# Two-layer hybrid decoder trunk on one core: value products issued for four attention units at a time in seven of sixteen steps

## The reference

```python
o = jnp.einsum('bngrqk,bnkgd->bnqgrd', (p / den).astype(v.dtype), vb)
```

## Time and profile before

| | us |
|---|---|
| three timed runs | 1310.58, 1310.74, 1311.07 (median 1310.74) |
| the profiled execution, its own time | 1306.06 |
| its span, first to last instruction | 1304.3 |

### The profile page before, as it was taken

How to read it: one execution, slowest core, us unless ns; L and a number is a source line. 1 busy time by engine, 2 the same in 40 slices (tenths; PEclk the granted TensorE clock), 3 DMA queues, 4 the chain that set the end, 5 groups by cost and what they waited for, 6 DMA issues and landing times.

```text
span 1304.3 us, 24577 instructions
## 1 busy us (share of the span) xinstructions
PE 1268.8 (97%) x8714; PEld 1182.7 (91%) x8714; DVE 763.3 (59%) x2339; ACT 643.5 (49%) x1777; POOL 368.9 (28%) x427
## 2 busy tenths in 40 slices
PE   4999999999999999999999999999999999999997
PEld 4998998988799999999989999899999899987997
DVE  5745453554772545666546666456775466668825
ACT  6445354454751445555446555456554456555312
POOL 2311142140301021212214932215832118610110
PEclk9999999999999999999999999999999999999999
DMA  5101012031546202101112311202310213215723
GB/s 203 39 19 50 26 54 85 18 98 37 173 148 202 98 25 54 40 25 25 51 50 65 86 58 36 65 26 83 98 44 19 65 39 91 84 31 138 212 98 129
DMA packets 101223, 97.29 MB, mean 75 GB/s; under 512 B 30704, under 2 KB 87536, under 8 KB 101104
## 3 DMA queue, kind: packets, MB, share of 16 engines
q1 hardware_dynamic: 101104, 95.73, 24.5%
HBM read 79.46 MB, written 16.25 MB: 73 GB/s over the span
## 4 chain that ended last, share of the span: by engine, by line
PE 85%; DVE 5%; issue 4%; DMA 3%; ACT 1%; SPq 1%; POOL 1%; DVEq 0%; ACTq 0%; POOLq 0%
PE j_bank L1162 59%; PE o_bank L1305 7%; PE t_bank L1284 6%; PE s_bank L1271 5%; PE j_bank L1249 3%; PE s_bank L1273 2%; DMA w_raw<-in_w_qkv 1%; PE o_bank L1162 1%; PE t_bank L1162 1%; DMA gate<-in_positions 1%; PE s_bank L1162 1%; DVE xr L1809 1%; DVE probs L1658 1%; DMA w_raw<-in_w_out 1%; DVE probs L1651 0%
## 5 line engine op out<-in xcount | busy, mean ns | idle before, releaser
L1162 PE MATMUL j_bank<-w_hi,ht_hi 128*128 128x384 f32 (+1 forms) x1312 | 445.0, 339 | 4.3 <-ACT v L1418 2.4
L1162 PE MATMUL j_bank<-w_lo,ht_hi 128*128 128x384 f32 (+1 forms) x1312 | 432.8, 330 | 0.0
L1162 PE MATMUL j_bank<-w_hi,ht_lo 128*128 128x384 f32 (+1 forms) x1312 | 432.7, 330 | 0.0
L1162 PEld LDWEIGHTS j_bank<-w_hi,ht_hi 128*128 128x128 f32 x1312 | 248.5, 189 | 16.2 <-issue 9.5
L1056 POOL TENSOR_TENSOR w_lo<-w_raw,w_hi 128x768 fp32r<-128x768 f32 (+1 forms) x60 | 104.6, 1744 | 550.9 <-ACT w_hi L1395 475.3
L1404 ACT ACTIVATE probs<-probs,stat 128x256 f32<-128x256 f32 (+1 forms) x512 | 231.0, 453 | 48.6 <-DVE stat L1663 46.7
L1162 PEld LDWEIGHTS j_bank<-w_lo,ht_hi 128*128 128x128 f32 x1312 | 248.8, 190 | 0.0
L1162 PEld LDWEIGHTS j_bank<-w_hi,ht_lo 128*128 128x128 f32 x1312 | 248.4, 189 | 0.0
L792 ACT COPY probs_t<-t_bank 128x256 f32<-128x256 f32 (+1 forms) x128 | 58.0, 453 | 282.2 <-PE o_bank L1305 276.5
L1395 ACT ACTIVATE w_hi<-w_raw 128x768 fp32r<-128x768 f32 (+1 forms) x120 | 88.5, 764 | 84.2 <-PE j_bank L1162 42.6
L1305 PE MATMUL o_bank<-probs_t,v 128*64 128x128 f32 x1600 | 116.4, 282 | 1.5 <-DVE probs_t L792 0.9
(11 more groups left out here) (170 smaller groups left out, 1849.4 us busy)
## 6 DMA issues: line engine op xcount, KB each, us to landing
w_raw<-in_w_qkv SPq DMA_DIRECT2D x64, 384.0 KB, 3.5
coef<-coef_dram SPq DMA_DIRECT2D x96, 128.0 KB, 3.0
w_raw<-in_w_gate SPq DMA_DIRECT2D x32, 256.0 KB, 3.3
mix_dram<-xr SPq DMA_DIRECT2D x12, 512.0 KB, 3.9
w_raw<-in_w_out SPq DMA_DIRECT2D x16, 384.0 KB, 3.7
qk<-mix_dram SPq DMA_DIRECT2D x12, 512.0 KB, 5.3
xr<-in_x SPq DMA_DIRECT2D x8, 512.0 KB, 7.2
out<-xr SPq DMA_DIRECT2D x7, 512.0 KB, 2.7
```

The source lines that it names most:

```text
L1162: last = pe.matmul(to, a(x_, kt), b(y_, kt), start=(start and kt == kts[0] and x_ == y_), stop=(stop and kt == kts[-1] and x_ == 1))
```

## The change

Three functions are added and two places use them.

- `by_fours(s)`: true for steps 0, 1, 2 (layer 0 without its last) and for steps 6, 9, 12, 15 (pattern 2).
- `values_at(s, a)`: which units get their value products in pair (s, a). For units of a step by fours, the pairs in which the older scheme would have taken units 0 and 1, 4 and 5, 8 and 9, or 12 and 13 take none, and the next pair takes all four. The products themselves, their order and their number stay.
- The copies of turned units need four places now. In pattern 2 only side 1 is used, so the unused half of `probs_t` serves (`own_place`). In layer 0 the two further places lie in `ot[3]` (`turned_place`).
- The copy's wait in such a step is for the unit four before it, not two. For the first two units of a pattern 2 step it stays at two.

The scores, transposes, fills, pieces, `store_ot`, all DMAs and all of DVE's, ACT's and POOL's instructions stay in number and order.

```diff
+def by_fours(s):
+    return s.p == 2 if s.layer == 1 else not s.last
+
+def values_at(s, a):
+    b, u = unit_before(s, a, V_BACK)
+    if b is None or (by_fours(b) and u % 4 == 0):
+        return []
+    return [(b, n) for n in range(u - 2 if by_fours(b) else u, u + 2)]
+
+def own_place(s, u):
+    return u // 2 % 2 if by_fours(s) and s.layer == 1 else 1
...
+        def turned_place(s, u):
+            if by_fours(s) and s.layer == 0 and u % 4 >= 2:
+                return ot[GROUPS - 1][:, 0, :].rearrange("p (a b c) -> p a b c", a=2, b=4)[:, u % 2, :, :]
+            return probs_t[:, u % 2, :, :]
+
...
-            if i >= 2:
+            if by_fours(s) and (u >= 4 or s.layer == 0):
+                if i >= 4:
+                    eng.wait_ge(summed, i - 3)
+            elif by_fours(s) and u >= 2:
+                eng.wait_ge(summed, UNITS * s.t + u - 3)
+            elif i >= 2:
                 eng.wait_ge(summed, i - 1)
...
-            to = probs_t[:, i % 2, :, :].rearrange("p (j e) q -> p j e q", e=2)
+            to = turned_place(s, u).rearrange("p (j e) q -> p j e q", e=2)
+            if by_fours(s) and s.layer == 1:
+                at = own_place(s, u)
+                return copy(to[:, :, at:at + 1, :], src[:, :, 1:2, :])
...
-                                         v[:, s.t % 2, n - 1 + side, :], probs_t[:, i % 2, 2 * j + side, :],
+                                         v[:, s.t % 2, n - 1 + side, :],
+                                         turned_place(s, u)[:, 2 * j + (own_place(s, u) if side == 1 else 0), :],
...
-                        for b, u in [unit_before(s, slot, V_BACK) for slot in pair]:
-                            if b:
-                                times_v(b, u)
+                        for b, u in values_at(s, a):
+                            times_v(b, u)
```

## The result

| | before | after |
|---|---|---|
| timed runs, median (lowest to highest) | 1310.66 (1310.21 to 1311.07, 4 runs) | 1301.52 (1300.11 to 1303.58, 4 runs) |
| the profiled execution, its own time | 1306.06 | 1303.58 |
| its span | 1304.3 | 1301.8 |
| granted clock over the span | 0.998 | 0.995 |

The ratio of the medians is 0.9932, 95% interval 0.9914 to 0.9949: faster, by little but clear of the noise. The forecast was 1304.9, range 1301.5 to 1308.0.

The account below looks back on a forecast made before the run. PE, busy 97% of the span, was taken as the bound: 8.8 us saved by 27 fewer blocks, less 2.3 at gate waits and 0.7 in step 15, gives 5.8, so 1310.74 becomes 1304.9; range 1301.5 to 1308.0.

Parts of the forecast that it names:

- price of a block: Each value-product block removed from PE saves 0.30 before a fill, 0.35 before a projection piece, 0.34 before a gate piece.
- number of blocks: 27 blocks of value products go: four in each of steps 0, 1, 2, 6, 9, 12 and three in step 15.
- rival A: All 8.8 us are kept, 1301.9, as the DMA lands earlier or DVE gets ahead in step 15; chance 0.12.
- rule of the Trainium skill: Changing tiling mode drains the engine, so every block costs the same two drains of 0.16: 8.6 us for 27 blocks.
- Small margins and ACT's waits: Reads before fills and pieces keep margins of 0.15, 0.40 and 0.23 in shortened pairs; costed at nothing.
- B: Rival: the nine small-margin pairs are pinned too; layer 1's pairs 4 and 0 give back 4.4 us, 1309.3; chance 0.11.
- C: Rival: copies waiting for blocks of four delay exponentials behind them in order, starving transposes; 5.5 us slower, 1316.2; chance 0.05.
- no waits for exponentials in the steps by fours: Sign to look for: in steps with four units per block, PE's transposes never wait for exponentials.
- Pairs (t, 12): In steps 6, 9, 12 the 0.78 saved lengthens PE's gate-piece wait while 0.44 moves to pair 14: 2.3 us lost.
- Step 15: Blocks of pairs 4 and 12 are lost in waits for DVE, 0.7 us in all; only pair 8's 0.34 counts.
- DVE sets the pace: In step 15, PE's waits for DVE's maxima in pair 8 absorb the 0.34 of pair 4's block.
- The clock stretch: In step 15 the granted clock is 0.50 for 3.40 us; a stretch more or less is worth up to 1.7 us.

Follow-up runs that it names:

- second trace of after: The changed kernel run again with no edit: 1302.08 (10 runs), 0.9956 against all runs of the kernel before beside it.
- experiment by ones: Kernel before with value products of layer 0's steps 0 to 2 in 48 blocks of one unit, not 24 of two: 1314.89, 1.0050.
- before again: The kernel before run once more with no edit: 1308.56 (12 runs), 1.0003.
- layer 0 alone: The change in layer 0's steps 0, 1 and 2 only, pattern 2 as in the kernel before: 1302.54, 0.9950 against before.
- places alone: The four places and their waits, but value products by twos in every pair as in the kernel before: 1307.0, 0.9990 against before.
- product moved: VectorE's product with the coefficients put behind the last copy at both layers' ends: after 1298.45, before 1305.67; in after at layer 0's end only, 1296.44.
- third trace of after: The changed kernel run a third time with no edit: 1300.56 (5 runs), 0.9925 against before.
- each layer alone: Two kernels, the change in layer 0's steps 0 to 2 only (1302.54, 0.9950) or in layer 1's pattern 2 only (1304.82, 0.9965), against before.
- pair 12 apart: The changed kernel with units 8 to 11 of steps 6, 9 and 12 by pairs again: 1300.71, 0.9937; with the product moved too, 1296.86.

## Why the prediction held, step by step

The mechanism held: the price of a block, the number of blocks, and the kind of wait that takes some of it back. The sum was too small by 1.6 us (5.8 forecast, 7.4 measured over all runs), and rival A's 1301.9, with a chance of 0.12, lay nearer to 1301.52 than the forecast did, though not for all of A's reasons.

- **Price of a block: right.** From (0, 4) to (3, 10), layer 0 has 12 blocks less in stretches with no wait. By the steps of the prediction that is 6 x 0.30 + 5 x 0.35 + 0.34 = 3.9; the trace shows 256.99 - 253.18 = 3.81 (3.85 in the second trace of after). The experiment by ones gives 0.30 from the other side. The moved products cost +0.43, the forecast 0.44.
- **The rule of the Trainium skill** ("TensorEngine Tiling (Array Packing)", Key Properties: a change of tiling mode drains the engine) names a cause that fits the runs: they show that the change of kind costs, and not what the array does in it. By the price worked out beside it, 0.16 a drain, the 12 blocks of layer 0 would give 12 x 2 x 0.16 = 3.8; by rows 3.9; measured were 3.81 and 3.85. The rows after don't tell the two apart.
- **Small margins and ACT's waits: right.** Waits for `v` read by ACT are 2.4 us, 7 times, before and after, and in steps 6, 9 and 12 each block taken from pairs (t, 4), (t, 8) and (t+1, 0) gives its full 0.31 to 0.33; B didn't come. Waits of transposes for exponentials are 1.1 us in all, as before, so C didn't either. The sign "no waits for exponentials in the steps by fours" wasn't met to the letter: step 15 has three of 0.28 to 0.29, where it had two before.
- **Pairs (t, 12): right in kind, too large in size.** The step that failed is "the 0.78 that the pair loses goes into a longer wait". The waits grew, but by 0.2 to 0.5. From (t, 4) to (t+1, 4) the six traces with before's order in layer 1 give 69.01 to 69.81, a mean of 69.16 over 18 values; the six with four units at a time in every second pair give 68.02 to 68.91, a mean of 68.33 over 18. That is 0.83 a step, against 0.51 forecast and 1.29 if nothing waited: 1.0 us more than forecast in three steps. Pair by pair, (t, 12) to (t, 14) is 0.33 shorter and (t, 14) to (t+1, 0) 0.43 longer on these means: the block costs 0.10 where 0.44 was forecast.

  The traces show why. In all 18 values without the block ACT's read of the gate piece starts 0.75 behind the start of its second `w_hi`, so it hangs on the DMA, as the prediction had it. With the block this holds for 11 of 18; in the other 7 the weights are there in time, ACT waits for the gate piece itself, and PE's wait is 0.25, as here in before again:

```profile
841.82 0.60 ACT L1422 ACTIVATE gate<-j_bank 128x512 f32<-128x512 f32 x1 [0.34 <-PE j_bank L1162]
842.47 0.50 PE L1162 MATMUL j_bank<-ht_hi,w_hi 128*128 128x512 f32 x1 [0.25 <-ACT gate L1422]
```

  There the pair can get shorter until the weights bind. The trace that the prediction read had all three waits on the DMA (0.79, 0.54, 0.40), and so showed no such room.
- **Step 15: one step right, one wrong, one missed.** Distances from each pair's first scores to the next's, and from (15, 14)'s to the first matmul behind the last value products:

| kernel | 4 to 6 | 6 to 8 | 8 to 10 | 10 to 12 | 12 to 14 | 14 to behind | sum |
|---|---|---|---|---|---|---|---|
| layer 0 alone | 5.61 | 4.99 | 5.91 | 4.52 | 4.55 | 8.78 | 34.36 |
| places alone | 5.64 | 4.97 | 5.91 | 4.52 | 4.55 | 8.15 | 33.74 |
| after | 4.82 | 5.79 | 5.08 | 4.95 | 3.75 | 8.71 | 33.10 |

  The wait in pair 8 takes 0.58 or 0.95 us in traces of either order; these three have 0.58, as here in after:

```profile
1184.41 0.51 PE L1307 MATMUL s_bank<-ks,qs 128*128 128x256 f32 x2 [0.58 <-DVE stat L1697]
1200.94 0.45 PE L1196 MATMUL s_bank<-w_hi,ht_hi 128*128 128x384 f32 x1 [0.49 <-DVE stat L1697]
```

  Right: "DVE sets the pace" in front of pair 8. From (15, 4) to (15, 8) it is 10.6 in all three, so the block of pair 4 gives nothing. The block of pair 8 gives 0.83 - 0.43 = 0.40, forecast 0.34. Wrong: the step that failed is that the block of pair 12 is lost in the wait of 0.36. The pair gets 0.80 shorter, 0.44 of it is paid in pair 14, and the wait grows only to 0.49, by 0.13: 0.2 are kept. Missed: 0.6 more come from the four places, which take away the wait for ACT's copy among the last value products (8.78 to 8.15, as shown with the places alone). Together that is 34.36 - 33.10 = 1.3 where 0.34 had been forecast. At the last matmul after is ahead of the other two by 1.4 and 1.1.
- **Pair (3, 10): missed.** (3, 10) to (3, 14) is 0.51 shorter. Before, transposes wait there for exponentials; after, they don't:

```profile
336.27 0.63 PE L1284 MATMUL t_bank<-ident,probs 128*128 128x128 f32 x4 [0.57 <-ACT probs L1404]
```
```profile
332.32 1.10 PE L1318 MATMUL t_bank<-ident,probs 128*128 128x128 f32 x6
```

  It goes with the length of pair (3, 2), which takes over a block: to the first scores of (3, 4) it is 5.67 before, 5.96 in units by ones, 6.55 after, and the wait is 0.57, 0.32 and none. ACT and DVE have the same work in all three and get ahead of PE while it is busy longer; the exponentials of (3, 10) stand 0.28 and 0.52 us earlier against its first scores. It isn't that ACT's copies wait less: with the places alone they do (139.5 us for products in place of 276.5), and the wait stays:

```profile
337.14 0.52 PE L1318 MATMUL t_bank<-ident,probs 128*128 128x128 f32 x3 [0.58 <-ACT probs L1438]
```

- **Layer 0's end: missed.** The prediction had no row of it. In it, PE waits for a DMA that hangs on POOL's products and two transfers, 3.1 to 4.4 us in the three traces of after and 2.9 to 3.6 in three of the four with before's order in layer 0 and nothing moved (0.90 in the fourth, the one that the prediction read). The stretch takes 153.6 on average in those four and 154.8 in the five with layer 0 by fours. Nearly all of this difference is the one trace with 150.39; the other three have 154.6. So the change loses between 0.2 and 1.2 us at this place, and the times don't settle it: the difference between the kernels is no larger with the product moved (7.2) than without (7.4).
- **The sum.** Measured by stretches: 3.8 + 0.5 in layer 0, 3 x 0.83 in steps 6, 9 and 12, 1.3 in step 15, that is 8.1, less 0.2 to 1.2 at layer 0's end: 6.9 to 7.9. The timed difference is 7.2 between the kernels with the product moved and 7.4 over all runs. The forecast of 5.8 was too small by 0.5 (pair (3, 10)), 1.0 (steps 6, 9 and 12) and 0.9 (step 15), and too large by what is lost at the end that it missed. Of the 3.4 us between 1304.9 and 1301.52, 1.6 are that the change brings 7.4 and not 5.8; the other 1.7 are that 1310.74 was 2.2 above before's median over all runs, and 1301.52 only 0.5 above after's.
- **The order of the queues.** Rival C asked what stands behind a waiting instruction only for the copies of the new order. The copy of unit 15 shows that for a DMA's wait. The Trainium skill states the rule ("TensorE: Matmul & The Clock Gate", Architectural detail: VectorE is strict first in, first out), and the trace agrees: PE's transposes of unit 15 end at 352.82 + 0.27 = 353.09, the copy starts at 358.27, behind the product that waited 5.95.
- **The clock stretch** was put in the range at up to 1.7 us, at step 15. It didn't show there in after, but at layer 0's end, for 6.8 us (3.4 in the third trace of after).

## What to carry to other kernels

Matmuls that use the array in another shape than their neighbours (here 128 x 64 among 128 x 128) cost 0.30 to 0.35 us each time the kind changes and back: group them as far as places for their inputs allow, and price it from the starts in a timeline. In a queue that is worked off in order, an instruction that waits for a DMA must not stand ahead of a ready copy that another engine needs: here moving one product was worth 3.6 to 4.1 us, about half as much as the whole change. Before a sum is made against one trace, look at a second one where there is one, or at least at each place where PE waits for a DMA: such waits differ between executions of one program (0.90 and 3.63 us at layer 0's end), and the trace read here had its three gate waits on late weights and its end of layer 0 on an early transfer.

## What the runs showed of the hardware

- Going back and forth between 128 x 128 and 128 x 64 operands costs the same whether blocks are added (0.30 for each of 24) or taken (0.30 to 0.35). Inside a block neither the input's place nor the number of units matters: 4, 8, 16 and 32 records take 0.37, 0.59, 1.02 and 1.90 to the next kind, 0.055 a record, and the change of place inside the 32 shows no gap.
- In eight traces with nothing moved (before again, after three times, each layer alone, places alone, pair 12 apart) a wait of PE of 2.9 to 4.4 us for unit 15 was followed by 3.4 or 6.8 us at a granted clock of 0.50. In two (before, by ones) the wait was 0.90 and 2.71 and the clock stayed at 1.00. In the four with the product moved there was no such wait, and the clock stayed at 1.00.
- The same program's layer 0 end took from 150.39 to 153.73 us in two executions, while the 257 us ahead of it repeated to 0.01.
- Ahead of that end one of POOL's last two products of 128 x 512 elements took 2.8 to 2.9 us in twelve traces, and in two both took 1.3. What lengthens it was not measured.
